# Latent attention in a streaming-encoder layer: scores and value products as three split products in place of native fp32 ones

## The reference

```python
sc = (jnp.einsum('bqhd,bkhd->bhqk', q_nope[:, q0:q1], k_nope[:, :k_end])
      + jnp.einsum('bqhr,bkr->bhqk', q_pe[:, q0:q1], k_pe[:, :k_end])).astype(jnp.float32) * scale
sc = jnp.where(k_chunk[None, :] <= q_chunk[:, None], sc, -jnp.inf)
p = jax.nn.softmax(sc, axis=-1).astype(v.dtype)
outs.append(jnp.einsum('bhqk,bkhd->bqhd', p, v[:, :k_end]))
```

## Time and profile before

| | |
|---|---|
| median of 3 runs | 1756.96 us (1756.79 to 1757.66) |
| the profiled execution | 1757.24 us, span in the trace 1755.4 us |
| PE busy | 1748.4 us, 100% of the span |
| DVE busy, ACT busy | 1113.3 us (63%), 932.8 us (53%) |
| granted TensorE clock | full (2.4 GHz level) in all 40 slices |
| the 8 passes of the attention | first query chunk at 83.9 us, last at 353.5 us (L451) |

### The profile page before, as it was taken

One profiled execution on the slowest core, in us unless ns is written; L12 is line 12 of the kernel. 1 busy time (PEld: TensorE's weight loads), 2 busy tenths in 40 slices (PEclk: granted clock), 3 DMA queues, 4 the chain that ended last, 5 costly groups with the idle time before them and its releaser, 6 DMA issues.

```text
span 1755.4 us, 25994 instructions
## 1 busy us (share of the span) xinstructions
PE 1748.4 (100%) x8758; PEld 1484.2 (85%) x8758; DVE 1113.3 (63%) x1541; ACT 932.8 (53%) x1262; POOL 5.6 (0%) x14
## 2 busy tenths in 40 slices
PE   9999999999999999999999999999999999999999
PEld 7888888888888888888888888888888888888887
DVE  6888876666755454545665666777666666755554
ACT  7765556656754444444664565555555555544443
POOL 0000000000000000000000000000000000000000
PEclk9999999999999999999999999999999999999999
DMA  8555454544455555556855455555555555565554
GB/s 321 189 173 173 163 170 160 165 160 150 153 178 190 192 190 191 191 192 216 308 184 189 146 168 192 191 185 187 190 187 189 186 188 185 188 200 195 191 191 155
DMA packets 90853, 329.75 MB, mean 188 GB/s; under 512 B 10128, under 2 KB 10384, under 8 KB 89776
## 3 DMA queue, kind: packets, MB, share of 16 engines
q1 hardware_dynamic: 89712, 321.96, 56.1%
q0 software_dynamic: 1088, 7.07, 1.0%
HBM read 326.83 MB, written 2.10 MB: 187 GB/s over the span
## 4 chain that ended last, share of the span: by engine, by line
PE 99%; DMA 0%; DVE 0%; ACT 0%; SPq 0%; issue 0%; ACTq 0%
PE ps L342 22%; PE ps L323 14%; PE ps L325 14%; PE ps L324 14%; PE ps L350 11%; PE ps L741 4%; PE ps L740 4%; PE ps L739 4%; PE ps L451 2%; PE ps L453 1%; PE ps L452 1%; PE ps L495 1%; PE ps L496 1%; PE ps L611 0%; PE ps L513 0%; DMA x_t<-in_x_t 0%
## 5 line engine op out<-in xcount | busy, mean ns | idle before, releaser
L1300 DVE TENSOR_TENSOR w_lo<-w_raw,w_hi 128x1024 fp32r<-128x1024 f32 x598 | 729.5, 1224 | 588.3 <-ACT w_hi L787 586.4
L787 ACT ACTIVATE w_hi<-w_raw 128x1024 fp32r<-128x1024 f32 x598 | 628.6, 1057 | 670.9 <-PE ps L325 334.5
L342 PE MATMUL ps<-u,w_hi 128*128 128x512 f32 x1664 | 422.1, 393 | 0.0
L342 PEld LDWEIGHTS ps<-u,w_hi 128*128 128x128 f32 x1664 | 297.9, 189 | 52.5
L323 PE MATMUL ps<-w_hi,u 128*128 128x512 f32 x608 | 242.3, 398 | 1.6 <-DVE w_lo L1337 1.4
L350 PEld LDWEIGHTS ps<-u,w_lo 128*128 128x128 f32 x1664 | 226.9, 190 | 16.4
L325 PE MATMUL ps<-w_hi,u 128*128 128x512 f32 x608 | 236.9, 390 | 0.0
L324 PE MATMUL ps<-w_lo,u 128*128 128x512 f32 x608 | 236.8, 389 | 0.0
L350 PE MATMUL ps<-u,w_lo 128*128 128x256 f32 x1664 | 231.9, 282 | 0.0
L323 PEld LDWEIGHTS ps<-w_hi,u 128*128 128x128 f32 x608 | 114.2, 188 | 27.2 <-issue 2.4
L325 PEld LDWEIGHTS ps<-w_hi,u 128*128 128x128 f32 x608 | 114.1, 188 | 24.2
(11 more groups left out here) (349 smaller groups left out, 1905.1 us busy)
## 6 DMA issues: line engine op xcount, KB each, us to landing
w_raw<-in_stream SPq DMA_DIRECT2D x600, 512.0 KB, 3.4
x_tok<-in_x SPq DMA_DIRECT2D x2, 1024.0 KB, 8.4
mem_raw<-in_mem_by_feature POOLq DMA_DIRECT2D x2, 1024.0 KB, 9.1
x_tok<-in_x POOLq DMA_DIRECT2D x2, 1024.0 KB, 7.8
mem_tok<-in_mem POOLq DMA_DIRECT2D x2, 1024.0 KB, 14.5
out<-x_tok SPq DMA_DIRECT2D x8, 256.0 KB, 3.2
x_t<-in_x_t SPq DMA_DIRECT2D x7, 256.0 KB, 5.3
w_raw<-in_stream SPq DMA_DIRECT2D x4, 256.0 KB, 4.9
```

The lines of the kernel that those rows point to most:

```text
L342: mm = pe.matmul(ps[:, bank + m, :], w_hi[:, s, lo:lo + P], act[:, kc, :, :].rearrange("p h t -> p (h t)"), start=(kc == 0), stop=(kc == K ...
L787: act.activation(w_hi[:, s, :], w_raw[:, s, :], ACT.Copy).then_inc(hi_made, 1)
L1300: TTo(w_lo[:, s, :], w_raw[:, s, :], w_hi[:, s, :].bitcast(F32), ALU.subtract).then_inc(lo_made, 1)
```

## The change

The operands of the scores and of the value products are held as a high part (fp32r) and a low part, and each native product becomes three fp32r products (`products`). The high parts lie where the fp32 tiles were. The low parts lie in the half of the output region that holds `y_b` later and is not in use during the attention. ACT makes all the high parts, one of which (`gk_hi`) DVE's copy was before; DVE makes the low parts by a subtraction that reads PSUM again. The shared rotary key is split once, ahead of the passes, and both its parts are copied to the other partitions. To stay within the number of semaphores, some pairs that counted two DMAs apart are one now (`memf_landed`, `x_again`, `mem_landed`), and `mem_squares(0)` moves from chunk 2 to chunk 4 of its block, which lies outside the attention.

```diff
@@ PE, mla_pass
                 pe.wait_ge(sem("mla_tok"), 4 * it + 4)
-                pe.wait_ge(sem("v_made"), it + 1)
+                pe.wait_ge(sem("g_lo"), 4 * it + 1)
...
-                pe.wait_ge(sem("gq_made"), 2 * it + 2)
-                pe.wait_ge(sem("gk_made"), it + 1)
-                pe.wait_ge(sem("kpe_copied"), 16)
+                def products(o, a, b, first=False, last=False):
+                    (a_hi, a_lo), (b_hi, b_lo) = a, b
+                    pe.matmul(o, a_hi, b_hi, start=first, stop=False, skip_group_check=True)
+                    pe.matmul(o, a_hi, b_lo, start=False, stop=False, skip_group_check=True)
+                    return pe.matmul(o, a_lo, b_hi, start=False, stop=last, skip_group_check=True)
+
+                pe.wait_ge(sem("g_lo"), 4 * it + 4)
+                pe.wait_ge(sem("kpe_copied"), 32)
...
-                        pe.matmul(o, gq[:, h, q], gk[:, h, keys], start=(t == 0), stop=False, skip_group_check=True)
-                        pe.matmul(o, gp[:, q], kpe[:, h, keys], start=False, stop=False, skip_group_check=True)
+                        products(o, [a[:, h, q] for a in (gq_hi, gq_lo)], [a[:, h, keys] for a in (gk_hi, gk_lo)],
+                                 first=(t == 0))
+                        products(o, [a[:, q] for a in (gp_hi, gp_lo)], [a[:, h, keys] for a in (kpe_hi, kpe_lo)])
@@ ACT, mla_pass
                 act.wait_ge(sem("mla_T"), 3 * it + 2)
-                act.activation(gp[:], ps[:, ATT + 1, 0:T], ACT.Copy).then_inc(sem("gq_made"), 1)
+                act.activation(gp_hi[:], ps[:, ATT + 1, 0:T], ACT.Copy).then_inc(sem("gq_made"), 1)
+                act.wait_ge(sem("mla_T"), 3 * it + 3)
+                act.activation(gk_hi[:].rearrange("p h t -> p (h t)"), ps[:, ATT + 2, :], ACT.Copy, scale=g_qk
+                               ).then_inc(sem("gk_made"), 1)
                 split(pos, 7)
...
                 act.wait_ge(sem("pT"), 2 * it + 2)
-                act.activation(prt[:, 1, :], ps[:, ATT + 2, 0:384], ACT.Copy).then_inc(sem("pt_1"), 1)
+                for h in range(2):
+                    act.activation(prt_hi[:, h, :], ps[:, ATT + 2 * h, 0:384], ACT.Copy).then_inc(sem("pt_hi"), 1)
@@ DVE, mla_pass
                 split(pos, 4)
+                dve.wait_ge(sem("v_made"), it + 1)
+                TTo(v_lo[:], heads(ps[:, ATT + 2:ATT + 4, T:2 * T]), v_hi[:].bitcast(F32), ALU.subtract).then_inc(sem("g_lo"), 1)
...
                 split(pos, 5)
+                dve.wait_ge(sem("gq_made"), 2 * it + 1)
+                TTo(gq_lo[:].rearrange("p h t -> p (h t)"), ps[:, ATT, :], gq_hi[:].rearrange("p h t -> p (h t)").bitcast(F32),
+                    ALU.subtract).then_inc(sem("g_lo"), 1)
                 split(pos, 6)
-                dve.wait_ge(sem("mla_T"), 3 * it + 3)
-                TS(gk[:].rearrange("p h t -> p (h t)"), ps[:, ATT + 2, :], g_qk, None, ALU.mult
-                   ).then_inc(sem("gk_made"), 1)
+                dve.wait_ge(sem("gq_made"), 2 * it + 2)
+                TTo(gp_lo[:], ps[:, ATT + 1, 0:T], gp_hi[:].bitcast(F32), ALU.subtract).then_inc(sem("g_lo"), 1)
+                dve.wait_ge(sem("gk_made"), it + 1)
+                STT(gk_lo[:].rearrange("p h t -> p (h t)"), ps[:, ATT + 2, :], g_qk,
+                    gk_hi[:].rearrange("p h t -> p (h t)").bitcast(F32), ALU.mult, ALU.subtract).then_inc(sem("g_lo"), 1)
                 split(pos, 7)
...
-                dve.wait_ge(sem("pT"), 2 * it + 2)
-                dve.wait_ge(sem("pt_1"), it + 1)
-                dve.tensor_copy(prt[:, 0, :], ps[:, ATT, 0:384]).then_inc(sem("pt_ready"), 2)
+                for h in range(2):
+                    dve.wait_ge(sem("pt_hi"), 2 * it + (h + 1))
+                    TTo(prt_lo[:, h, :], ps[:, ATT + 2 * h, 0:384], prt_hi[:, h, :].bitcast(F32), ALU.subtract
+                        ).then_inc(sem("pt_ready"), 1)
```

More of the change, by code:

```diff
@@ L140, in build @@
                     [("y_a", [P, KC, 2, T], F32R), ("y_b", [P, KC, 2, T], F32R)],
-                    [("rb_pad", [P, 8192], F32), ("qa_t", [P, LC, 2, T], F32R), ("kv_t", [P, LC, 2, T], F32R)],
+                    [("rb_pad", [P, 8192], F32), ("qa_t", [P, LC, 2, T], F32R), ("kv_t", [P, LC, 2, T], F32R),
+                     ("gq_lo", [P, 2, T], F32R), ("gk_lo", [P, 2, T], F32R), ("gp_lo", [P, T], F32R),
+                     ("kpe_lo", [P, 2, T], F32R), ("v_lo", [P, TT, 2, P], F32R), ("prt_lo", [P, 2, 384], F32R)],
                     [("mem_t", [P, KC, 2, T], F32R), ("mem_tok", [P, TT, D], F32), ("mem_raw", [P, KC, T], F32)],
@@ L147, in build @@
         y_a, y_b, qa_t, kv_t, mem_t = rb["y_a"], rb["y_b"], rb["qa_t"], rb["kv_t"], rb["mem_t"]
+        gq_lo, gk_lo, gp_lo, kpe_lo, v_lo, prt_lo = (
+            rb[n] for n in ("gq_lo", "gk_lo", "gp_lo", "kpe_lo", "v_lo", "prt_lo"))
         mem_tok, mem_raw, ck, cv, cq, c_sq, c_p, c_pt, h_ff = (
@@ L165, in build @@
              ("r0_bc", [P, 1, T], F32)],
+            [("hi_pad0", [P, zv_b // 4 + 16 * T], F32), ("kpe_hi", [P, 2, T], F32R), ("hi_pad1", [P, 2 * T], F32),
+             ("gq_hi", [P, 2, T], F32R), ("gk_hi", [P, 2, T], F32R), ("gp_hi", [P, T], F32R),
+             ("hi_pad2", [P, 7 * T], F32), ("v_hi", [P, TT, 2, P], F32R), ("hi_pad3", [P, 3 * T], F32),
+             ("prt_hi", [P, 2, 384], F32R)],
             [("mpad", [P, zv_b // 4 + 16 * T + 5 * T], F32),
@@ L512, in mla_pass @@
                     o = ps[:, A3, h * T:(h + 1) * T]
-                    pe.matmul(o, v_pair[:, 0, h, :], prt[:, h, 0:T], start=(h == 0), stop=False,
-                              skip_group_check=True)
-                    mm = pe.matmul(ps[:, A3, h * T + P:(h + 1) * T], v_pair[:, 1, h, :], prt[:, h, T:T + P],
-                                   start=False, stop=True, skip_group_check=True)
+                    products(o, [a[:, 0, h, :] for a in (v_hi, v_lo)], [a[:, h, 0:T] for a in (prt_hi, prt_lo)],
+                             first=(h == 0))
+                    mm = products(ps[:, A3, h * T + P:(h + 1) * T], [a[:, 1, h, :] for a in (v_hi, v_lo)],
+                                  [a[:, h, T:T + P] for a in (prt_hi, prt_lo)], last=True)
                 mm.then_inc(sem("attended"), 1)
@@ L794, in mem_high @@
             def mem_high(i):
-                act.wait_ge(sem(f"memf_landed{i // 4}"), 16)
+                act.wait_ge(sem("memf_landed"), 32)
                 for kc in (2 * i, 2 * i + 1):
@@ L975, in mla_pass @@
                 act.activation(pr[:, :, 0:T], ps[:, ATT + 2:ATT + 4, 0:T], ACT.Square).then_inc(sem("sqk_made"), 1)
-                act.activation(v_pair[:], heads(ps[:, ATT + 2:ATT + 4, T:2 * T]), ACT.Copy).then_inc(sem("v_made"), 1)
+                act.activation(v_hi[:], heads(ps[:, ATT + 2:ATT + 4, T:2 * T]), ACT.Copy).then_inc(sem("v_made"), 1)
                 act.wait_ge(sem("ms_made"), 3 * it + 3)
@@ L982, in mla_pass @@
                 act.wait_ge(sem("mla_T"), 3 * it + 1)
-                act.activation(gq[:].rearrange("p h t -> p (h t)"), ps[:, ATT, :], ACT.Copy).then_inc(sem("gq_made"), 1)
+                act.activation(gq_hi[:].rearrange("p h t -> p (h t)"), ps[:, ATT, :], ACT.Copy).then_inc(sem("gq_made"), 1)
                 split(pos, 5)
@@ L1118, in _ @@
                         mem_high(MEM_AT[n][c])
-                    if n == 1 and c in (2, 6):
-                        mem_squares(c // 4)
+                    if n == 1 and c in (4, 6):
+                        mem_squares(c // 5)
                     if n == 2 and c == 0:
@@ L1462, in _ @@
                 if c == 2:
-                    dve.memset(kpe[ROPE:2 * ROPE, 0, :], 0.0).then_inc(sem("kpe_made"), 1)
-                    dve.memset(kpe[0:ROPE, 1, :], 0.0).then_inc(sem("kpe_made"), 1)
+                    for a in (kpe_hi[:].bitcast(F32), kpe_lo[:].bitcast(F32)):
+                        dve.memset(a[ROPE:2 * ROPE, 0, :], 0.0)
+                        ins = dve.memset(a[0:ROPE, 1, :], 0.0)
+                    ins.then_inc(sem("kpe_made"), 1)
                     TTo(g_qk, col("g_qn_nope"), col("g_kn_nope"), ALU.mult)
```

35 lines of the change are left out of this document (19 added, 16 removed).

## The result

The changed kernel takes **1760.97 us** (median of 15 runs, 1760.60 to 1761.45). The kernel before, run beside it, takes 1757.11 us (15 runs, 1756.79 to 1757.68). The ratio is 1.0022, 95% interval 1.0014 to 1.0029: 3.9 us, 0.22% slower. The forecast was 1762.0 us, so the sign and the range hold and the time was forecast 1.0 us too long (the terms summed to +5.1 us, +3.9 were measured). The profiled execution of after has a span of 1759.4 us, that of before 1755.4.

The account below looks back on a forecast made before the run. The prediction took PE to bound the kernel, DVE and ACT counting only where PE waits. Terms 2.6 + 2.4 + 0.1 = +5.1 us on 1757.24 gave 1762.3, forecast as 1762.0 us (8-in-10 range 1757.5 to 1772).

Parts of the forecast that it names:

- PE is the bound: Whole kernel: an added or removed matmul moves the end; DVE or ACT work counts only where PE waits for it.
- The wait before the scores, +2.4 us: Scores' start: `gp_lo` delays the last operand by 0.34 us, so PE waits 0.30 us in each of eight passes.
- the cover: Scores' start, kernel before: 0.04 us between the first load being good and the end of the previous matmul's stream.
- PE's own work, +2.6 us: Score and value products: 3.90 us a pass becomes 4.23, so +0.33 us in each of 8 passes.
- The lower end: Score and value products: +1.9 us in 8 passes if a 128-column fp32r matmul takes 0.11 us.
- The rule of four passes: fp32 products: native takes four array passes, so three cost three quarters; at most 7.8 us gained, 1749.2 us.
- `y_a`, +0.1 us: Pass end: low part of `y_a` comes 0.14 us later; PE's wait grows 0.03 to 0.1 us, three times.
- The rest at nothing: Key's split ahead of the passes and merged DMA semaphores: costed at nothing.
- Wait absent: Scores' start: no wait or only the split's lower end, 1758.9 to 1760.1 us; chance 0.13.
- Quarter rate: 128-column products: narrow fp32r matmuls run at a quarter of the rate, 1778.6 us; chance 0.12.
- Loads shared by a stationary tile: Product triples: matmuls in a row on one stationary tile need no new load, 1751.7 to 1754.1 us; chance 0.07.
- More waits: Later passes: spare time before `split(pos, 6)` used up, or pass ends back up, 1765 to 1772 us; chance 0.06.

Follow-up runs that it names:

- products only: Changed kernel with its three fp32r matmuls per product reading high parts alone, DVE and ACT working as in the kernel before: 1758.15 us, 1.0006 of the kernel before.
- Low parts alone: Changed kernel with ACT's and DVE's work kept, but one native fp32 product on the high tiles, low parts unmultiplied: 1759.47 us, 1.0014 of the kernel before.

## Why the prediction was right, and where it was off

- **PE is the bound, and distances between starts carry the cost.** Right. Every difference above is a sum of such distances; the busy time of PE grew by 4.1 us, which here agrees by luck.
- **The wait before the scores, +2.4 us.** Right in place, cause and size: 0.27 us in pass 0 (0.30 forecast); over 8 passes after less products only, 3.11 - 0.82 = 2.29 us. Low parts alone bring it (+2.24), and one operation less takes it away. The load starts 0.06 us behind `gk_lo` (0.08 forecast). That DVE's work ahead of `split(pos, 6)` is free and its work behind it is not held for `v_lo`, `gq_lo` and `gp_lo`; the two `prt_lo` take 0.47 us each, as forecast, and PE doesn't wait for them. That the cover was 0.04 us could only be read from the starts, and what I didn't look at is that it was gone before the change in passes 3 and 7.
- **PE's own work, +2.6 us.** The term that was mis-sized. The mechanism is right (wide products cheaper, narrow ones dearer, one load each), the stretches give 0.82 + 0.5 = 1.3 us, below 0.2 us a pass in place of 0.33. I took 0.115 us for a narrow matmul and a rounded 0.12 for a wide one; neighbours are 0.112 and 0.117 us apart (medians of the trace), so 18 x 0.112 + 18 x 0.117 = 4.12 instead of 4.23, 0.22 a pass. A difference of two sums of 4 us, from rows rounded to 0.01, needs the third digit. And I counted eight passes of value products where the last one's cost goes into the wait behind it. What is left, some 0.04 us a pass, isn't assigned. The lower end that I gave for this term (1.9 us, at 0.11) was the nearer one.
- **The rule of four passes.** Measured, three fp32r products take 3 x 0.117 / 0.43 = 0.82 of a native one with 256 columns and 3 x 0.112 / 0.22 = 1.5 times it with 128. By the Trainium skill ("FP8 and Floating Point Precision", TensorE Precision Notes) a true fp32 product takes four passes through the array, from which I had worked out three quarters. The trace comes near that with 256 columns and disagrees with 128, where the load is the limit. For the load the runs show 0.112 and 0.060 us (distance between starts, stationary tiles of 128 and 64 columns) and 0.106 to 0.109 and 0.058 us (time per matmul added). By a section of the Trainium skill that I didn't weigh ("TensorE: Matmul & The Clock Gate", LDWEIGHTS (loading the stationary operand)), a load takes the columns of the stationary tile divided by 1.2, in ns, which is 107 ns for 128 and 53 for 64. The runs agree with that.
- **`y_a`, +0.1 us.** Right: the -0.09 in the stretch is +0.1 once the border is set right, and the loader waits 0.34, 0.34 and 0.41 us in place of 0.30, 0.30 and 0.38. DVE is delayed a little more than PE. So small a term can't be told from the timed runs, only from these rows. Its other face I didn't see: whatever shortens PE's work at a pass's end is partly lost at this wait, 0.33 of 1.5 us in the run with native value products.
- **The rest at nothing.** Held; no new wait on DMA or on the merged semaphores is in the trace, and behind the first pass's start the stretches outside the passes' changed parts are within 0.05 us. The time up to it varies by more, for kernels with the same code there.
- **Rivals.** Wait absent: refuted, 8 waits. Quarter rate: refuted, 0.112 us apart where 0.23 was needed. Loads shared by a stationary tile: refuted, 8854 loads for 8854 matmuls, and 12 times the same tile in a row still costs 0.106 each. More waits: no new one; `split(pos, 6)` kept its wait in pass 4 (0.15 us, forecast 0.13 to spare).

So of 3.9 us, 2.3 are one subtraction in a place without cover, 1.3 are dearer products and 0.1 is `y_a`; the last 0.2 is within what the time to the first pass varies by. The forecast came out near because the wait was right; the other large term, 2.6, was twice what it measured.

## What to carry to other kernels

Splitting an fp32 product in three pays here only when its moving side has 256 columns (0.35 for 0.43 us); with 128 it costs half as much again, since each matmul brings a load of 0.11 us and only 0.06 us of stream to hide the next one under. So split wide products and leave narrow ones native: with both, and two DVE orders turned, the same idea is 4.1 us faster than the kernel before instead of 3.9 slower. Before adding an operation to a helper engine, find the last operand that PE waits for and put nothing, above all no unrelated chunk, between its input and it; and when PE gets faster, look at which wait it reaches early. A wait further on also takes in what a change costs or gives: the eighth pass's value products got dearer in one kernel and cheaper in another, and the 4.50 us from there to the next waiting matmul stayed.

## What the runs showed of the hardware that I had not expected

- A narrow fp32r matmul between wide ones is no cheaper than in a row (0.108 and 0.106 us). Its own columns take 0.06 us, and the rest shows up at its neighbour, which takes 0.28 in place of 0.23 us. By these rows a load hides only under the matmul just ahead of it.
- Moving columns below 128 change nothing (64: 0.109 us each), columns of the stationary tile do (64: 0.058 us each). In these runs the time of a narrow product goes by the operand that is held, not by the one that streams.
- A native fp32 product of 128 columns is two instructions 0.11 us apart, each with a load. That is two loads against the split's three, and this is why it beats them. Whether its loads or its streams set the 0.11 isn't shown: one instruction of 256 columns takes 0.22 us, so half of that is as long as a load.
